# Rotary swap of the retention branch: ScalarE copies between partition quarters instead of permutation products on TensorE

## Chip, cores and metric

The kernel runs on one core of one Trainium2 chip. The metric is the device time of one execution in microseconds (us); the kernel before has a median of 1391.2 us over 3 runs.

## What is computed

Two blocks run one after the other on a sequence of 256 tokens of width 1024, all in float32. The first block is attention beside a recurrence, then a mixture of 32 experts. The second block, where the change lies, has two layers; each projects the normed state into 12 slices of 256 channels, runs four mixers on them and then a feed-forward network:

```python
for l in range(2):
    h = rms_norm(x, norm_mix_pre[l])
    (c_a, c_gate, sb_q, sb_k, sb_v, r_q, r_k, r_v, r_g, sc_b, sc_c, sc_h) = split(h @ w_in[l], 12)
    mix = concat([conformer_conv(c_a, c_gate), stick_breaking_attention(sb_q, sb_k, sb_v),
                  retention(r_q, r_k, r_v, r_g), short_gated_conv(sc_b, sc_c, sc_h)]) @ w_out[l]
    x = x + rms_norm(mix, norm_mix_post[l])
    x = x + rms_norm(conv_ffn(rms_norm(x, norm_ffn_pre[l])), norm_ffn_post[l])

def rotary(x, pos):                      # on r_q and r_k, per head of 64 channels
    x1, x2 = x[..., :32], x[..., 32:]
    return concat([x1 * cos - x2 * sin, x2 * cos + x1 * sin])
```

Channels lie on partitions, so a head's 64 channels are two quarters of 32 partitions. The rotary turn needs `x * cos + swap(x) * sin`, where swap exchanges the two quarters of each head and negates the one that lands in the lower.

## The kernel before

The program is written by hand for each engine (TensorE PE, VectorE DVE, ScalarE ACT, SyncE SP), each with its own list of instructions in the order of the code; semaphores tie them. `layers_part` holds the two layers.

**Projections.** The weight matrices come in pieces of 1 MB (128 partitions x 2048). For each piece ACT rounds the raw weights to `w_hi` (`split_piece`, L2842), DVE makes the rest `w_lo` (`split_low`, L3048), and PE makes a product from `w_hi`*`x_hi`, `w_hi`*`x_lo`, `w_lo`*`x_hi` (`product`, L2700; `values_product`, L2712, for the two v slices; `tokens_product`, L2736, for the output matrix). Piece i uses half-slot i mod 3, so ACT may split piece i when PE has finished piece i-3. Inside a product the part with `w_lo` comes last.

**Order on PE in a layer.** conf_a, conf_gate, sb_q, sb_k, ret_q, the scores of the stick-breaking attention (L2651, L2652), ret_k, ret_v, the two swaps (L2761), the attention's tail sums (L2767 to L2769), sb_v, retention scores from the turned q and k (L2651, L2652 on `o_T`), sc_c, attention output (L2663), sc_h, retention output, sc_b, the group sums ret_mean (L2784), ret_g, ret_var (L2788), conf_mean (L2792), and then the output matrix in rows of pieces (L2736), with conf_var (L2807) after the first.

**The swap.** `m.c("swap")` is a 128x128 permutation with signs; `pe.matmul(ps[b], swap, s_[name])` writes the swapped q or k (128x512) to a PSUM bank. DVE multiplies it with sin (L3112), the slice with cos (L3113), and adds (L3115) into `turned` (the tile `o_T`). Both are done for q, then for k; the second ends with the count 2 of `turned`, for which the retention scores wait. After the turn of k DVE goes on to the tail (L3119), `split_low(8)`, taps of the convolution (L3059), the mask of the retention scores (L3127, L3128), `split_low(9)` for sc_h, and so on.

**PSUM banks.** There are 8 banks of 128x512. `_units` gives every product of a layer a bank before anything runs: the first ones by hand, the middle ones, from conf_gate to conf_var, from a running number n mod 8, and the output matrix and the feed-forward network by hand again:

```python
    for name, count in (("conf_gate", 1), ("sb_q", 1), ("sb_k", 1), ("vec", 1), ("ret_q", 1),
                        ("sb_score", 4), ("ret_k", 1), ("ret_v", 1), ("swap", 2), ("tail", 4), ("sb_v", 1),
                        ...
        for k in range(count):
            use((name, k), n % BANKS)
            n += 1
    for n in range(4):
        use(("out", n), 3 + n)
```

PE calls `free(name)` before it writes a bank; that waits until whoever read the bank's previous use has raised `drained` of the bank (in the listings below `bank_drained2_N`, and `bank_filled2_N` for the count that PE raises). Before the output matrix PE waits for all four of its banks at once: `banks = [free("out", n) for n in range(4)]`. By the table these banks were last used as follows:

| bank of the output matrix | last used by | drained by |
|---|---|---|
| 3 (out 0) | ret_out 0 | ACT copy L2934 |
| 4 (out 1) | ret_out 1 | ACT copy L2934 |
| 5 (out 2) | sc_b | DVE L3158 |
| 6 (out 3) | ret_mean | DVE L3152 |

**ACT between ret_g and the output matrix.** After the product ret_g ACT copies it through SiLU (L2829), loads the table set for Ln and Exp (`preload_act_table_set`, L2939), splits piece 14 (L2842), takes the logarithm of ret_var out of PSUM (L2942), which drains that bank, squares the centred convolution (L2945), and exponentiates (L2947).

## Time and profile before

| | |
|---|---|
| median of 3 runs | 1391.2 us (1389.97 to 1391.92) |
| the profiled execution | 1390.5 us |
| its span, first to last instruction | 1388.6 us |
| instructions | 22573 |
| PE busy | 1186.8 us (85%), 9519 matmuls |
| PEld busy (weight loads, beside PE) | 947.1 us (68%) |
| DVE busy | 743.7 us (54%) |
| ACT busy | 490.3 us (35%) |
| chain that ended last | PE 59%, DMA 16%, DVE 2%, issue 2% |
| layers, from first product to end | 768 to 1388 us |
| mixer of layer 0, of layer 1 | 774 to 881 us, 1082 to 1189 us |

The profile is one execution. Its span leaves out some 2 us around the first and the last instruction. A row of the timeline gives a start, a duration, the engine, line and tiles of a group of like instructions; ends of matmuls are modelled and overlap the next start by about 0.2 us, so distances between starts are what counts on PE. "PEclk" is the clock that TensorE was granted as a share of 2.4 GHz. The experts in the middle of the kernel (340 to 765 us) wait for weights from memory; the layers behind them are ruled by PE.

### The profile page before, as it was taken

Reading aid. Unit: us, or ns where it says so; the run is one execution under the profiler, and the core shown is the slowest. Engines: PE = TensorE matmul, PEld = TensorE weight load, DVE = VectorE, ACT = ScalarE, POOL = GpSimd, SP = SyncE. Lnnn points to the kernel's source line nnn. Section 1 sums busy time; section 2 is a strip of 40 time slices with the busy share of each in tenths; the row PEclk is TensorE's granted clock in tenths of the full one; section 3 lists DMA queues with packets and bytes.
Section 4 is the critical chain, followed back from the end, with each engine's and each line's share of the span. In section 5 each row is a group of like instructions: output and inputs, shape, how many; then the busy total and the mean of one; then the engine's idle time right before and its main releaser. Section 6 shows DMA issues by size and latency. Waiting matters only on the chain.

```text
span 1388.6 us, 22573 instructions
## 1 busy us (share of the span) xinstructions
PE 1186.8 (85%) x9519; PEld 947.1 (68%) x9519; DVE 743.7 (54%) x1148; ACT 490.3 (35%) x674; POOL 2.9 (0%) x12
## 2 busy tenths in 40 slices
PE   7989999999574575736656999999999999999998
PEld 6979798995131221302122898899998998899997
DVE  5484855664010110101001798887777899877776
ACT  4542433422000000000000655744446565744444
POOL 0000000000000000000000000000000000000000
PEclk9999999999786877868688999999999999999999
DMA  8841303799999999999999934576665435676650
GB/s 264 283 132 35 92 4 93 251 404 370 426 427 427 425 426 427 426 426 427 426 425 399 300 123 142 163 216 190 186 182 182 140 119 159 187 204 191 187 152 31
DMA packets 180986, 349.50 MB, mean 252 GB/s; under 512 B 8141, under 2 KB 154738, under 8 KB 167955
## 3 DMA queue, kind: packets, MB, share of 16 engines
q1 hardware_dynamic: 180394, 347.40, 68.9%
q8 instruction: 78, 1.28, 0.4%
q10 hardware_dynamic: 488, 0.62, 0.2%
q14 instruction: 26, 0.21, 0.0%
HBM read 346.93 MB, written 3.43 MB: 252 GB/s over the span
## 4 chain that ended last, share of the span: by engine, by line
PE 59%; DMA 16%; DVE 2%; issue 2%; SPq 1%; ACT 1%; DVEq 1%; ACTq 0%
PE ps L2700 25%; PE ps L2736 11%; DMA expert_ring<-in_w_expert_up 7%; PE ps L1900 6%; DMA expert_top<-in_w_expert_up 4%; PE ps L1931 3%; DMA expert_early<-in_w_expert_up 2%; PE ps L1585 2%; DMA expert_ring<-in_w_expert_gate 2%; PE ps L1888 2%; PE ps L1945 2%; PE ps L2712 2%; PE ps L2674 2%; DMA expert_ring<-in_w_expert_down 1%; SPq L2035 1%
## 5 line engine op out<-in xcount | busy, mean ns | idle before, releaser
L1900 PE MATMUL ps<-expert_ring,w_slot 128*32 128x512 f32 x640 | 118.0, 730 | 101.8 <-DMA expert_ring<-in_w_expert_gate 48.0
L3048 DVE TENSOR_TENSOR w_lo<-expert_early,w_hi 128x2048 fp32r<-128x2048 f32 x80 | 182.8, 2291 | 26.1 <-ACT w_hi L2842 22.8
L1973 DVE TENSOR_TENSOR hT<-ps,hT 128x512 f32<-128x512 f32 x8 | 8.5, 1068 | 346.3 <-PE ps L1900 346.3
L2842 ACT ACTIVATE w_hi<-expert_early 128x2048 fp32r<-128x2048 f32 x80 | 153.0, 1918 | 56.5 <-PE ps L2736 33.8
L1900 PEld LDWEIGHTS ps<-expert_ring,w_slot 128*32 128x32 f32 x640 | 30.8, 131 | 168.9 <-issue 168.9
L2700 PE MATMUL ps<-x_hi,w_hi 128*128 128x256 f32 x960 | 134.2, 282 | 0.0
L2700 PE MATMUL ps<-x_hi,w_lo 128*128 128x256 f32 x960 | 134.2, 282 | 0.0
L2700 PE MATMUL ps<-x_lo,w_hi 128*128 128x256 f32 x960 | 132.3, 280 | 0.0
L2700 PEld LDWEIGHTS ps<-x_hi,w_hi 128*128 128x128 f32 x960 | 122.9, 188 | 3.8 <-issue 1.6
L2700 PEld LDWEIGHTS ps<-x_hi,w_lo 128*128 128x128 f32 x960 | 123.0, 190 | 0.0
L2700 PEld LDWEIGHTS ps<-x_lo,w_hi 128*128 128x128 f32 x960 | 121.0, 188 | 0.0
L3224 DVE SCALAR_TENSOR_TENSOR ff<-ps,ff_taps,ff 128x254 f32<-128x254 f32 (+1 forms) x176 | 76.7, 477 | 47.3 <-ACT ff L2982 43.3
L2982 ACT ACTIVATE ff<-ps,ff_taps 128x256 f32<-128x256 f32 x88 | 36.9, 471 | 118.3 <-PE ps L2700 117.5
L1900 PE MATMUL ps<-expert_early,w_slot 128*32 128x512 f32 x192 | 52.7, 711 | 22.2 <-DMA expert_ring<-in_w_expert_gate 12.6
L1952 ACT ACTIVATE hT<-ps 128x512 f32<-128x512 f32 x8 | 4.8, 597 | 173.0 <-PE ps L1910 173.0
L1900 PE MATMUL ps<-const,w_slot 128*32 128x512 f32 x48 | 37.4, 952 | 32.4 <-DMA expert_early<-in_w_expert_up 21.5
L1950 ACT ACTIVATE hT<-ps 128x512 f32<-128x512 f32 x8 | 4.8, 597 | 154.2 <-PE ps L1900 154.2
L1900 PE MATMUL ps<-expert_top,w_slot 128*32 128x512 f32 x96 | 58.1, 773 | 0.0
L3059 DVE SCALAR_TENSOR_TENSOR att_T<-conf_pad,vec,att_T 128x256 f32<-128x256 f32 x120 | 52.8, 481 | 4.2 <-issue 0.4
L1931 PE MATMUL ps<-expert_ring,hT 128*32 128x512 f32 x288 | 44.3, 620 | 8.7 <-issue 7.3
L2736 PE MATMUL ps<-w_hi,hid_lo 128*128 128x512 f32 x176 | 48.9, 396 | 0.0
L2736 PE MATMUL ps<-w_lo,hid_hi 128*128 128x512 f32 x176 | 48.8, 396 | 0.0
(516 smaller groups left out, 2146.4 us busy)
## 6 DMA issues: line engine op xcount, KB each, us to landing
expert_ring<-in_w_expert_gate SPq DMA_DIRECT2D x22, 2048.0 KB, 28.8
expert_ring<-in_w_expert_up SPq DMA_DIRECT2D x18, 2048.0 KB, 30.0
expert_early<-in_ffn_up SPq DMA_DIRECT2D x36, 1024.0 KB, 6.1
expert_ring<-in_w_expert_down SPq DMA_DIRECT2D x14, 2048.0 KB, 29.8
w_slot<-in_w_in SPq DMA_DIRECT2D x27, 1024.0 KB, 5.5
expert_early<-in_w_in SPq DMA_DIRECT2D x20, 1024.0 KB, 5.6
expert_early<-in_ffn_down SPq DMA_DIRECT2D x18, 1024.0 KB, 5.0
expert_early<-in_w_expert_gate SPq DMA_DIRECT2D x6, 2048.0 KB, 27.5
```

Of the source, the lines that this page charges most:

```text
L1585: mm = pe.matmul(out, w[:, pair_of(i), col:col + P], x[y][:, x0 + k, :], start=(p == 0 and k == 0), stop=(p == 2 and k == n - 1))
L1888: mm = pe.matmul(m.ps[:, b, c * P:(c + 1) * P], m.h_tok[:, t, (4 * j + c) * P:(4 * j + c + 1) * P], picked[:, t, :], start=(t == 0), stop= ...
L1900: mm = pe.matmul(m.ps[rows_of(e), b, :], x_quad[:, k, rows_of(e)], w[e][:, k, :], start=(k == 0), stop=(k == KC - 1))
L1931: mm = pe.matmul(m.ps[rows_of(e), DOWN + j, :], hidden_T[:, f, rows_of(e)], w[e][:, f, j * 512:(j + 1) * 512], start=(f == 0), stop=(f == ...
L1945: pe.matmul(m.ps[:, b, :], gate_T[:, q // 2 * P:(q // 2 + 1) * P], y_quad[:, q % 2 * 512:(q % 2 + 1) * 512], start=True, stop=True).then_i ...
L2700: mm = pe.matmul(m.ps[:, b, j * SEQ:(j + 1) * SEQ], w[:, s, at(k, j):at(k, j) + P], x[:, k, :], start=(part == 0 and k == 0), stop=(part = ...
L2736: mm = pe.matmul(m.ps[:, banks[2 * t + c], :], xs[:, chunk + k, t * P:(t + 1) * P], w[:, s, k * D + c * 512:k * D + (c + 1) * 512], start= ...
L2842: act.activation(w_hi[:, half_slot(l, i), :], raw_slot(m, i), ACT.Copy).then_inc(S["w_hi"], 1)
L2982: ins = act.activation(ff[:, n % 2, j, :], m.ps[:, b, at:at + SEQ], ACT.Copy, scale=ff_taps[:, 2, j * FF + n:j * FF + n + 1])
L3048: dve.tensor_tensor(w_lo[:, s, :], raw_slot(m, i), w_hi[:, s, :].bitcast(F32), ALU.subtract).then_inc(S["w_lo"], 1)
L3059: dve.scalar_tensor_tensor(conf[:, c, :], src, tap, conf[:, c, :], ALU.mult, ALU.add)
L3224: ins = dve.scalar_tensor_tensor(x, m.ps[:, b, at:at + SEQ - back], ff_taps[:, 2 - back, j * FF + n:j * FF + n + 1], x, ALU.mult, ALU.add)
```

## The change

The two swap products leave PE, and their two entries leave the table of banks. ACT makes the swap instead: four activations of 32 partitions x 512 for q after the copy of ret_k, four for k after the copy of ret_v, each from one quarter of the slice to the neighbouring one, with the factor -1 where it lands in a lower quarter. DVE reads the new SBUF tile `swapped` instead of a bank, and waits for the count `swapped`.

```diff
--- before.py
+++ after.py
@@ -2374,7 +2374,7 @@
         use(("conf_a", j), 3 + j)
     n = 1
     for name, count in (("conf_gate", 1), ("sb_q", 1), ("sb_k", 1), ("vec", 1), ("ret_q", 1),
-                        ("sb_score", 4), ("ret_k", 1), ("ret_v", 1), ("swap", 2), ("tail", 4), ("sb_v", 1),
+                        ("sb_score", 4), ("ret_k", 1), ("ret_v", 1), ("tail", 4), ("sb_v", 1),
                         ("ret_score", 4), ("sc_c", 1), ("sb_out", 2), ("sc_h", 1), ("ret_out", 2), ("sc_b", 1),
                         ("ret_mean", 1), ("ret_g", 1), ("ret_var", 1), ("conf_mean", 1), ("conf_var", 1)):
         for k in range(count):
@@ -2501,6 +2501,7 @@
     ret_rs = sb("ret_rs", [P, 2, SEQ])
     ret_o = sb("ret_o", [P, 2, SEQ])
     ret_sq = sb("ret_sq", [P, 2, SEQ])
+    swapped = sb("swapped", [P, 2, 2, SEQ])
     s_ = {n: slices[:, i, :, :] for i, n in enumerate(KEPT)}
 
 
@@ -2512,7 +2513,7 @@
 
     total = {"x_ready": 4, "root": 8, "sum_squared": 8, "scaled": 4, "vec_set": 1, "h_hi": 16, "h_lo": 16, "w_hi": PIECES,
              "w_lo": PIECES, "out_used": 3, "down_used": 10, "y_split": 4, "conf_done": 1,
-             "conf_centred": 1, "conf_squared": 1, "conf_out": 1, "turned": 2, "sb_biased": 4, "soft_ln": 4, "sb_masked": 4,
+             "conf_centred": 1, "conf_squared": 1, "conf_out": 1, "turned": 2, "swapped": 2, "sb_biased": 4, "soft_ln": 4, "sb_masked": 4,
              "sb_arg": 4, "sb_exp": 4, "ret_masked": 4, "ret_centred": 1, "ret_squared": 1, "conf_rooted": 1,
              "ret_rooted": 1, "tap_scaled": FF, "conv_done": FF, "silu_done": FF, "hid_done": FF,
              "conf_normed": 1, "x_half": 2, "half_squared": 2, "half_eps": 2}
@@ -2755,10 +2756,6 @@
             masked_scores("sb_score", s_["sb_k"], s_["sb_q"])
             project("ret_k")
             project("ret_v")
-            for i, name in enumerate(("ret_q", "ret_k")):
-                await_drained(pe, l, name)
-                b = free("swap", i)
-                pe.matmul(m.ps[:, b, :], m.c("swap"), s_[name], start=True, stop=True).then_inc(filled[b], 1)
             if l == 0:
                 pe.wait_ge(m.const_late, 16)
             for h in range(4):
@@ -2913,10 +2910,24 @@
             act.drain()
             for h in range(4):
                 act.activation(sb_l[:, h, :], sb_l[:, h, :], ACT.Ln, bias=1.0).then_inc(S["soft_ln"], 1)
+            def swap_halves(i, name):
+
+                if l > 0:
+                    signalled(act, l - 1, "turned", 2)
+                for r in range(0, P, 32):
+                    low = r % HEAD == 0
+                    src = r + 32 if low else r - 32
+                    ins = act.activation(swapped[r:r + 32, i, :, :], s_[name][src:src + 32, :, :], ACT.Copy,
+                                         scale=-1.0 if low else 1.0)
+                ins.then_inc(S["swapped"], 1)
+
             split_piece(7)
             copy(s_["ret_k"], "ret_k")
+            act.drain()
+            swap_halves(0, "ret_q")
             split_piece(8)
             copy(s_["ret_v"], "ret_v")
+            swap_halves(1, "ret_k")
             split_piece(9)
             for h in range(4):
                 signalled(act, l, "sb_arg", h + 1)
@@ -3108,8 +3119,8 @@
             split_low(7)
             cos, sin = (m.c(n).rearrange("p (o t) -> p o t", o=1).to_broadcast([P, 2, SEQ]) for n in ("cos", "sin"))
             for i, name in enumerate(("ret_q", "ret_k")):
-                b = await_filled(dve, l, "swap", i)
-                dve.tensor_tensor(turn_tmp[:, :, :], two(m.ps[:, b, :]), sin, ALU.mult).then_inc(drained[b], 1)
+                signalled(dve, l, "swapped", i + 1)
+                dve.tensor_tensor(turn_tmp[:, :, :], swapped[:, i, :, :], sin, ALU.mult)
                 dve.tensor_tensor(turned[:, i, :, :], s_[name], cos, ALU.mult)
                 dve.drain()
                 dve.tensor_tensor(turned[:, i, :, :], turned[:, i, :, :], turn_tmp[:, :, :], ALU.add)
```

How the instructions stand. In the listings `bank_drained2_N` and `bank_filled2_N` are the counts of bank N; names such as `rstd_done` or `a_rstd` are those under which an earlier part used the same semaphore, here the layer's own counts (`sb_masked`, `y_split`, `w_hi` and their like).

TensorE at the swap of layer 0, before (the last products are those of ret_v; L2767 to L2769 are the tail):

```order
L2712 MATMUL ps<-w_hi,x_lo 128x256 x8
L2712 MATMUL ps<-w_lo,x_hi 128x256 x8
L2761 MATMUL ps<-slices,const 128x512 [waits bank_drained2_4,bank_drained2_5]
L2761 MATMUL ps<-slices,const 128x512 [waits bank_drained2_5,bank_drained2_2]
L2767 MATMUL ps<-sb_l,const 128x256 [waits bank_drained2_6,rstd_done,const_late]
L2768 MATMUL ps<-sb_l,const 128x128
L2769 MATMUL ps<-sb_l,const 128x128
L2767 MATMUL ps<-sb_l,const 128x256 [waits bank_drained2_7,rstd_done]
```

and with the change:

```order
L2713 MATMUL ps<-w_hi,x_lo 128x256 x8
L2713 MATMUL ps<-w_lo,x_hi 128x256 x8
L2764 MATMUL ps<-sb_l,const 128x256 [waits bank_drained2_4,x_squared,const_late]
L2765 MATMUL ps<-sb_l,const 128x128
L2766 MATMUL ps<-sb_l,const 128x128
L2764 MATMUL ps<-sb_l,const 128x256 [waits bank_drained2_5,x_squared]
```

Two rows with L2761 are gone, and the tail's products go to banks 4 and 5 where they had 6 and 7.

ScalarE at the same place, before (`w_hi` rows split pieces 7, 8 and 9; `slices` rows copy ret_k and ret_v):

```order
L2842 ACTIVATE w_hi<-expert_early 128x2048 [waits bank_filled2_5,landed2_2]
L2829 ACTIVATE slices<-ps 128x512 [waits bank_filled2_2]
L2842 ACTIVATE w_hi<-expert_early 128x2048 [waits bank_filled2_2,landed2_3]
L2829 ACTIVATE slices<-ps 128x512 [waits bank_filled2_3]
L2842 ACTIVATE w_hi<-w_slot 128x2048 [waits bank_filled2_3,landed2_4]
L2923 ACTIVATE w_slot<-w_slot 128x384 [waits x_squared] x4
```

and with the change:

```order
L2839 ACTIVATE w_hi<-expert_early 128x2048 [waits bank_filled2_5,landed2_2]
L2826 ACTIVATE slices<-ps 128x512 [waits bank_filled2_2]
L2920 ACTIVATE swapped<-slices 32x512 x4
L2839 ACTIVATE w_hi<-expert_early 128x2048 [waits bank_filled2_2,landed2_3]
L2826 ACTIVATE slices<-ps 128x512 [waits bank_filled2_3]
L2920 ACTIVATE swapped<-slices 32x512 x4
L2839 ACTIVATE w_hi<-w_slot 128x2048 [waits bank_filled2_3,landed2_4]
L2934 ACTIVATE w_slot<-w_slot 128x384 [waits rows_zero] x4
```

Two groups of four copies stand in; pieces 8 and 9 are split behind them.

TensorE from the variance of retention to the output matrix, layer 0, before:

```order
L2700 MATMUL ps<-x_hi,w_lo 128x256 x8
L2788 MATMUL ps<-ret_sq,const 128x512 [waits bank_drained2_0,vec_in]
L2792 MATMUL ps<-att_T,const 128x256 [waits bank_drained2_1,pads_zero]
L2792 MATMUL ps<-att_T,const 128x256
L2736 MATMUL ps<-w_hi,x_hi 128x512 [waits bank_drained2_6,line_out,bank_drained2_5,a_rstd,bank_drained2_4,bank_drained2_3]
L2736 MATMUL ps<-w_hi,x_hi 128x512 x3
```

and with the change:

```order
L2701 MATMUL ps<-x_hi,w_lo 128x256 x8
L2785 MATMUL ps<-ret_sq,const 128x512 [waits bank_drained2_6,const_in]
L2789 MATMUL ps<-att_T,const 128x256 [waits bank_drained2_7,pads_zero]
L2789 MATMUL ps<-att_T,const 128x256
L2737 MATMUL ps<-w_hi,x_hi 128x512 [waits bank_drained2_6,line_out,bank_drained2_5,a_rstd,bank_drained2_4,bank_drained2_3]
L2737 MATMUL ps<-w_hi,x_hi 128x512 x3
```

The order is the same. What moved is the bank of ret_var: its matmul waited for bank 0 and now for bank 6, and the first product of the output matrix waits, as before, for banks 3 to 6.

ScalarE over the same stretch, before:

```order
L2829 ACTIVATE slices<-ps 128x512 [waits bank_filled2_7]
L2939 ACT_TABLE_LOAD
L2842 ACTIVATE w_hi<-w_slot 128x2048 [waits bank_filled2_7,landed2_4]
L2942 ACTIVATE ret_rs<-ps,const 128x512 [waits bank_filled2_0]
L2945 ACTIVATE conf_sq<-att_T 128x512 [waits w1_lo_done]
```

and with the change:

```order
L2826 ACTIVATE slices<-ps 128x512 [waits bank_filled2_5]
L2950 ACT_TABLE_LOAD
L2839 ACTIVATE w_hi<-w_slot 128x2048 [waits bank_filled2_5,landed2_4]
L2953 ACTIVATE ret_rs<-ps,const 128x512 [waits bank_filled2_6]
L2956 ACTIVATE conf_sq<-att_T 128x512 [waits w1_lo_done]
```

The order is the same; the logarithm of ret_var (`ret_rs<-ps,const`) reads bank 6 where it read bank 0, and it is what drains the bank.

## Rows read from the trace of the kernel before

**Rows 1.** Window, mixer of layer 0: us, busy PE, PEld, DVE, ACT, POOL; PEclk, DMA

```profile
770.00:858.00 88.00, 87.10 (x710) 82.84 (x709) 77.92 (x127) 48.25 (x56) 0.00 (x0) 1.00 0.55 178
```

**Rows 2.** Chain of waits at the swap, both layers: start, us, what

```profile
816.54 1.72 PE ps L2761 x4
...
1124.50 1.72 PE ps L2761 x4
```

**Rows 3.** Timeline of ACT at the swap, layer 0; copy of ret_k, layer 1

```profile
814.33 0.57 ACT L2829 ACTIVATE slices<-ps 128x512 f32<-128x512 f32 x1
...
823.57 0.53 ACT L2923 ACTIVATE w_slot<-w_slot 128x384 f32<-128x384 f32 x1 [4.58 <-DVEq L3121]
...
1121.83 0.57 ACT L2829 ACTIVATE slices<-ps 128x512 f32<-128x512 f32 x1
```

**Rows 4.** Timeline of ACT, prices: four of 384 elements, one of 512

```profile
809.00 1.77 ACT L2912 ACTIVATE sb_l<-sb_l 128x384 f32<-128x384 f32 x4
...
851.81 0.63 ACT L2937 ACTIVATE ret_sq<-ret_o 128x512 f32<-128x512 f32 x1
```

**Rows 5.** Timeline of DVE: turn of k in both layers, then w_lo for sc_h

```profile
820.76 0.69 DVE L3112 TENSOR_TENSOR turn_tmp<-ps,const 128x512 f32<-128x512 f32 x1
...
834.78 2.29 DVE L3048 TENSOR_TENSOR w_lo<-w_slot,w_hi 128x2048 fp32r<-128x2048 f32 x1
...
1128.60 0.69 DVE L3112 TENSOR_TENSOR turn_tmp<-ps,const 128x512 f32<-128x512 f32 x1 [0.47 <-issue]
...
1142.62 2.29 DVE L3048 TENSOR_TENSOR w_lo<-w_slot,w_hi 128x2048 fp32r<-128x2048 f32 x1
```

**Rows 6.** Timeline of PE: first use of that w_lo in sc_h, both layers

```profile
838.42 1.12 PE L2700 MATMUL ps<-x_hi,w_lo 128*128 128x256 f32 x8
...
1146.38 1.12 PE L2700 MATMUL ps<-x_hi,w_lo 128*128 128x256 f32 x8
```

**Rows 7.** Timeline of DVE where it waited for PE: sc_pad, and splitting y

```profile
842.48 0.69 DVE L3136 TENSOR_TENSOR sc_pad<-ps,slices 128x512 f32<-128x512 f32 x1 [0.32 <-PE ps L2700]
...
856.33 0.43 DVE L3035 CAST x_hi<-hT 128x512 fp32r<-128x512 f32 x1 [0.81 <-PE ps L2700]
```

**Rows 8.** Timeline of PE before the output matrix, layer 0, then layer 1

```profile
856.99 1.02 PE L2792 MATMUL ps<-att_T,const 128*128 128x256 f32 x4
857.78 1.17 PE L2736 MATMUL ps<-w_hi,x_hi 128*128 128x512 f32 x4
...
1165.73 1.17 PE L2736 MATMUL ps<-w_hi,x_hi 128*128 128x512 f32 x4
```

**Rows 9.** Timeline of ACT from the copy of ret_g to Ln, both layers

```profile
856.33 0.60 ACT L2829 ACTIVATE slices<-ps 128x512 f32<-128x512 f32 x1 [2.58 <-PE ps L2700]
856.94 1.28 ACT L2939 ACT_TABLE_LOAD   x1
858.24 1.92 ACT L2842 ACTIVATE w_hi<-w_slot 128x2048 fp32r<-128x2048 f32 x1
860.06 0.67 ACT L2942 ACTIVATE ret_rs<-ps,const 128x512 f32<-128x512 f32 x1
...
1168.02 0.67 ACT L2942 ACTIVATE ret_rs<-ps,const 128x512 f32<-128x512 f32 x1
```

**Rows 10.** Windows over pauses of PE and what followed, columns as in rows 1

```profile
100.70:103.30 2.60, 0.00 (x0) 0.00 (x0) 2.56 (x2) 0.00 (x0) 0.00 (x0) 1.00 0.01 2
103.30:108.50 5.20, 5.18 (x27) 4.72 (x27) 4.88 (x9) 0.00 (x0) 0.00 (x0) 0.67 0.17 28
...
138.90:140.40 1.50, 0.02 (x1) 0.05 (x1) 0.42 (x2) 0.06 (x1) 0.06 (x1) 1.00 0.38 40
140.40:145.00 4.60, 4.60 (x22) 4.06 (x23) 4.43 (x6) 2.16 (x3) 0.25 (x1) 1.00 0.64 215
286.20:288.40 2.20, 0.01 (x2) 0.01 (x1) 2.04 (x4) 1.62 (x1) 0.00 (x0) 1.00 0.98 417
288.40:292.50 4.10, 4.10 (x22) 4.10 (x22) 3.93 (x5) 0.00 (x0) 0.00 (x0) 0.58 1.03 440
```

## Prediction, made before the changed kernel was timed

> **What bounds the kernel here.** I read the page first: shares of busy time and the chain that ended last. The layers come after the experts, and in that chain they are one piece of PE work after another. So I cut out the mixer. Over 88 us of layer 0 PE is busy for 87.1, DVE for 77.9 and ACT for 48.3, at the full clock [rows 1]. PE is the bound, DVE runs close behind it, ACT has room. The chain of waits says the same of the swap: its products lie on the path with 1.72 us in each layer [rows 2]. What is taken from PE is gained in full only as long as DVE and ACT, and the PSUM banks that they give back, are never late. So I went through the timeline of all three engines behind the swap, and through every wait of PE there by the table of banks.
>
> **What goes.** Two products of 128x512 in each layer, four matmul records, 1.72 us on the chain [rows 2]: 2 x 1.72 = 3.4 us, if nothing takes their place. DVE's multiplication with sin reads SBUF instead of PSUM. That costs nothing either way, since the row from PSUM takes 0.69 us and the reader is not at fault for the wait that follows.
>
> **What comes on ACT.** Eight activations of 32 partitions x 512 per layer. No row shows one that crosses partition quarters. The nearest: one of 512 elements takes 0.63 us, and four of 384 take 1.77 us, so 0.41 from start to start with 0.53 for the last [rows 4]. The 0.10 us between 0.53 and 0.63 goes on top of the step: 0.52. A group of four is then 3 x 0.52 + 0.63 = 2.2 us. From below I take the step of the 384 row (1.8 us), from above four with no overlap (2.5 us), and I stay with 2.2, which comes from rows of the same engine and length. Fewer partitions I count as no saving.
>
> These 2 x 2.2 us fit into ACT's idle time. Behind these splits ACT waited 4.58 us for DVE [rows 3]. But the group for k comes late: the copy of ret_k ends at 814.90 [rows 3], then group q to 817.1, the split of piece 8 (1.92 us, the row of such a split in rows 9) to 819.0, the copy of ret_v to 819.45, group k to 821.55, each start overlapping the end before by 0.1. DVE began the turn of k at 820.76 [rows 5]; now it waits until about 821.57, **0.8 us late**. In layer 1 the copy of ret_k starts at 1121.83 [rows 3], 307.5 later, so group k ends at 1129.05, and DVE, which began at 1128.60 [rows 5], is **0.5 us late**. Queued behind that wait on DVE are the tail, w_lo of sc_c, taps, the masks and w_lo of sc_h; none can be skipped, and DVE has no idle time in between.
>
> **First place where that meets PE: sc_h.** w_lo of sc_h was done at 834.78 + 2.29 = 837.07 [rows 5], and PE first used it at 838.42 [rows 6]: 1.35 us of slack. PE now comes 1.72 earlier (836.70) and w_lo 0.8 later (837.87). With 0.05 us for the signal PE waits 1.2 and keeps 0.5 of its 1.72. In layer 1 w_lo was done at 1144.91 and used at 1146.38 [rows 5, 6]: now 1145.4 against 1144.66, a wait of 0.8, and 0.9 is kept. The same comparison at sc_c, the product before it, where the slack was 3.0 us, leaves 0.5. The retention scores need both turns at about 825.7 and have them at 823.7.
>
> **Second place: the output matrix, by way of the banks.** Taking two entries out of a running number mod 8 moves every later product two banks down, while the output matrix keeps banks 3 to 6 by hand. ret_var had bank 0 and now has bank 6, which is bank "out 3". PE asks for all four banks before the first row of the output matrix, and bank 6 is now given back by ACT's logarithm of ret_var. Both PE and ACT start from the same event here, the end of the product ret_g. PE came to the output matrix at 857.78 [rows 8]. ACT copies ret_g at 856.33, loads a table (1.28), splits piece 14 (1.92), and ends the logarithm at 860.06 + 0.67 = 860.73 [rows 9]. With the signal PE can start at 860.78, so it waits **3.0 us** more than before. In layer 1 the logarithm ends at 1168.69 and PE came at 1165.73 [rows 8, 9]: 3.0 again. Nothing that is gained ahead of ret_g helps, since the race begins at its end. DVE's work for the first row of the matrix was due before that and gets slack from it; after it PE runs as before, and the rest of the layer hangs on PE.
>
> The table load stands in this race. Its row shows 1.28 us with the next instruction 0.02 later [rows 9]. The Trainium skill (ScalarE: Activation LUTs, "What ACT_TABLE_LOAD costs") puts a drain of about 1.38 us behind every load. By that the logarithm would end some 1.4 us later, and the sum below would be 2.7 us higher. The row shows no such drain, so it is left out.
>
> **Third: TensorE's clock.** PE's last product before the matrix ends at 858.01 [rows 8], so the new pause is 860.78 - 858.01 = 2.8 us. The trace has two pauses of like length: 2.6 us, after which the granted clock averaged 0.67 over 5.2 us, and 2.2 us, after which it was 0.58 over 4.1 us; after one of 1.5 us it stayed at 1.00 [rows 10]. A fall is to 1.2 of 2.4 GHz, and costs 5.2 x 0.33 = 1.7 us or 4.1 x 0.42 = 1.7 us of PE's work. The new pause is longer than both that were followed by a fall, so I count **1.7 us** per layer. From below it is nothing, if the fall does not come.
>
> **The sum.** Layer 0: -1.72 + 1.2 + 3.0 + 1.7 = +4.2. Layer 1: -1.72 + 0.8 + 3.0 + 1.7 = +3.8. Together **+8.0 us**. The profiled execution took 1390.5 us (span 1388.6), so it would become 1398.5. The median shown is 1391.2, 0.7 above it, and on that footing the time is **1399.2 us**, 0.6% slower. With groups of 1.8 us DVE is not late: 1.3 and 1.4 us are kept and the sum is +6.7. With 2.5 us DVE is 1.4 and 1.1 late: PE's waits at sc_h are 1.8 and 1.4, nothing and 0.3 are kept, and the sum is +9.2. So the forecast's own range is 1398 to 1400.4, and 1397 to 1401 with the scatter of a median of three.
>
> **Rivals.**
> (1) *The bank wait, but no fall of the clock.* For it: the layers show no fall at all so far [rows 1], and whether one comes may depend on more than the length of the pause. Against: both longer pauses of rows 10 were followed by one. +8.0 - 3.4 = +4.6, so 1395.8. One fall of two gives 1397.5.
> (2) *The other side: bank 6 is free in time.* The mechanism is the cover behind ret_g. If ACT's logarithm ended 3.0 us sooner after ret_g, PE would not stop, and there would be no pause for the clock either. For it: rows 2, where the gain is plain. Against: the chain of four instructions in rows 9 has no idle time to shrink, and the listing shows the wait on bank 6 in front of the matrix. It decides when copy, load, split and logarithm take under 1.65 us together, where the rows have 4.4. Then 0.5 + 0.9 us stay, 1389.8, or a little less, because DVE had only 0.32 + 0.81 us of idle time to give up [rows 7] before its splitting of y holds PE. If ACT's copies cost DVE nothing either, the gain is 1.3 + 1.4 = 2.7 us, and 1387.8 where sc_h has slack too.
> (3) *Copies between quarters are dearer than any row here.* One us more per group makes DVE 2 us later in each layer and sc_h waits 2 longer: +4 us, 1403. Against: the rows of ACT go by elements per partition, and nothing in them speaks of where a result lands.
> That the swap's products stay on PE after all is excluded by the listing.
>
> **How the numbers follow.** Forecast 0.74; no fall, or one of two, 0.13; copies much dearer 0.05; bank free in time 0.08. A measurement of this kernel can tell about 0.2%, 2.8 us, from no change. Slower by more than that: the first three, 0.92. Within it: 0.05, and faster 0.03, the two parts of rival 2. The range goes from below rival 1 to the top of the forecast: 1395.2 to 1401.2; outside it lie rivals 2 and 3, 0.13, and little of the rest.
>
> **What the profile after would show.** In each layer, a new idle time of about 2.8 us on PE in front of L2737, released by ACT's `ret_rs` (L2953); behind it a stretch of PEclk at half; a wait of about 1 us in sc_h for w_lo; DVE waiting 0.4 to 0.8 us for ACT at the turn of k; groups of four on ACT of 2.2 us. I am wrong if PE has no idle time before the output matrix, or if the clock holds over it.

## The result, and the profile after

The changed kernel took 1403.7 us (1399.05 to 1404.46, 5 runs) where the kernel before, on the same chip, took 1391.92 us (1389.97 to 1392.85, 5 runs): a ratio of 1.0082 with an interval from 1.0071 to 1.0092, slower. A second set of 6 runs of it gave 1401.1 us and 1.0067 (1.0052 to 1.0081). The forecast was 1399.2 with a range up to 1401.2. So the direction was right and the size too small: by 4.5 us against the first median, which lies outside the range, and by 1.9 against the second, which lies just inside it.

The profiled execution took 1401.57 us, which is 11.1 above that of before (1390.5). The page of the kernel after (busy time and instructions of each engine; the chain that ended last):

```profile
span 1399.7 us, 22571 instructions
...
PE 1187.8 (85%) x9511; PEld 949.4 (68%) x9511; DVE 744.0 (53%) x1148; ACT 500.5 (36%) x690; POOL 2.9 (0%) x12
...
PE 50%; DMA 16%; DVE 6%; ACT 3%; issue 3%; DVEq 2%; SPq 1%; ACTq 0%
```

ACT carries 10.2 us more (490.3 before), which is four groups of four copies at 2.55. PE has eight matmul records fewer and is yet not less busy. Part of the chain has moved from PE (59% before) to DVE and ACT (2% for DVE before): PE now waits for them.

**Where the time went.** I cut each layer's mixer at four points of PE's timeline that both kernels have: the start of the layer (its products with `scale_eye`, which transpose the state), the start of ret_var, the first row of the output matrix, and the end of that matrix. Times in us, layer 0 / layer 1, from the starts of the rows:

| stretch of PE | before | after | difference | predicted |
|---|---|---|---|---|
| A: first product to ret_var | 86.79 / 85.70 | 87.42 / 86.17 | +0.63 / +0.47 | -0.5 / -0.9 |
| B: ret_var to the output matrix | 1.65 / 1.64 | 4.95 / 4.96 | +3.30 / +3.32 | +3.0 / +3.0 |
| C: the output matrix | 23.47 / 23.56 | 24.84 / 24.92 | +1.37 / +1.36 | +1.7 / +1.7 |

That is +10.5 us in the mixers, where the forecast had +8.0. The rest of the 11.1 is nearly all ahead of the layers (0.55 us, in code that did not change). The evidence follows, stretch by stretch.

**Stretch A.** ACT's timeline at the swap of layer 0, and the group for q in layer 1 (start, us, engine, line, tiles, count of instructions in the row, idle time before it and what ended it):

```profile
814.89 0.57 ACT L2826 ACTIVATE slices<-ps 128x512 f32<-128x512 f32 x1
815.54 2.55 ACT L2920 ACTIVATE swapped<-slices 32x512 f32<-32x512 f32 x4
818.11 1.91 ACT L2839 ACTIVATE w_hi<-expert_early 128x2048 fp32r<-128x2048 f32 x1
819.93 0.58 ACT L2826 ACTIVATE slices<-ps 128x512 f32<-128x512 f32 x1
820.53 2.55 ACT L2920 ACTIVATE swapped<-slices 32x512 f32<-32x512 f32 x4
...
1128.69 2.55 ACT L2920 ACTIVATE swapped<-slices 32x512 f32<-32x512 f32 x4 [0.36 <-issue]
```

A group takes 2.55 us, not 2.2: four times 0.64 one behind the other. It does not overlap its neighbours either: the split starts at 818.11, 0.02 after the group's end, and the second group 0.02 after the end of the copy. The starts of ret_k's copy lie where they did ([rows 3] plus the 0.55 us from before the layers). On DVE the turn of k then waits:

```profile
823.11 0.69 DVE L3123 TENSOR_TENSOR turn_tmp<-swapped,const 128x512 f32<-128x512 f32 x1 [1.91 <-ACT swapped L2920]
...
837.14 2.29 DVE L3059 TENSOR_TENSOR w_lo<-w_slot,w_hi 128x2048 fp32r<-128x2048 f32 x1
...
844.44 0.69 DVE L3147 TENSOR_TENSOR sc_pad<-ps,slices 128x512 f32<-128x512 f32 x1
...
1136.28 0.69 DVE L3123 TENSOR_TENSOR turn_tmp<-swapped,const 128x512 f32<-128x512 f32 x1 [2.20 <-ACT swapped L2920]
```

The turn of k began at 820.76 before [rows 5]; with 0.55 us for the code ahead of the layers that is 821.31, so DVE is 1.8 us late. It is still 1.8 late at w_lo of sc_h (834.78 in rows 5, plus 0.55, against 837.14). The idle time that DVE had before sc_pad [rows 7] is used up. PE meets this twice in each layer, in sc_c and in sc_h:

```profile
830.42 1.22 PE L2701 MATMUL ps<-x_hi,w_lo 128*128 128x256 f32 x8 [0.34 <-DVE w_lo L3059]
...
839.49 1.21 PE L2701 MATMUL ps<-x_hi,w_lo 128*128 128x256 f32 x8 [1.42 <-DVE w_lo L3059]
...
1143.59 1.21 PE L2701 MATMUL ps<-x_hi,w_lo 128*128 128x256 f32 x8 [0.19 <-DVE w_lo L3059]
...
1152.66 1.21 PE L2701 MATMUL ps<-x_hi,w_lo 128*128 128x256 f32 x8 [1.42 <-DVE w_lo L3059]
```

Of the 1.72 us that left PE, none is kept. A group of eight that starts after a wait has its next group 1.05 us behind it instead of 0.95, and the idle time shown is less than the gap between starts, since ends of matmuls are modelled. Starts are the safe reading.

**Stretch B.** PE before the output matrix, layer 0, then layer 1:

```profile
857.32 1.02 PE L2785 MATMUL ps<-ret_sq,const 128*128 128x512 f32 x2
858.18 1.03 PE L2789 MATMUL ps<-att_T,const 128*128 128x256 f32 x4
862.27 1.70 PE L2737 MATMUL ps<-w_hi,x_hi 128*128 128x512 f32 x4 [3.07 <-ACT ret_rs L2953]
863.78 1.91 PE L2737 MATMUL ps<-w_hi,x_lo 128*128 128x512 f32 x4
...
1175.45 1.18 PE L2737 MATMUL ps<-w_hi,x_hi 128*128 128x512 f32 x4 [3.07 <-ACT ret_rs L2953]
```

and ACT's chain that ends the wait:

```profile
857.52 0.60 ACT L2826 ACTIVATE slices<-ps 128x512 f32<-128x512 f32 x1 [1.82 <-PE ps L2701]
858.13 1.28 ACT L2950 ACT_TABLE_LOAD   x1
859.43 1.91 ACT L2839 ACTIVATE w_hi<-w_slot 128x2048 fp32r<-128x2048 f32 x1
861.24 0.67 ACT L2953 ACTIVATE ret_rs<-ps,const 128x512 f32<-128x512 f32 x1
```

The four instructions are those of [rows 9] with the same durations, and the logarithm's end, 861.91, releases PE. Behind the table load the next instruction starts 0.02 us after its end, as it did before. The drain of some 1.38 us that the Trainium skill (ScalarE: Activation LUTs, "What ACT_TABLE_LOAD costs") adds to a load is again not seen, neither there nor ahead of the load, which starts 0.01 us after the end of the copy. PE does not start 0.05 us after the logarithm but 0.36.

**Stretch C.** The granted clock in a window of 6 us behind the start of the output matrix, each layer (us, then busy time of PE, PEld, DVE, ACT, POOL, then PEclk, DMA share, GB/s):

```profile
862.00:868.00 6.00, 5.72 (x18) 4.59 (x19) 5.70 (x8) 1.07 (x2) 0.00 (x0) 0.72 0.81 221
1176.00:1182.00 6.00, 6.00 (x21) 4.76 (x20) 4.99 (x7) 0.32 (x1) 0.00 (x0) 0.72 0.94 262
```

The granted clock averaged 0.72 in both, where the kernel with the banks put back, below, has 1.00: it fell in both layers. The rows of four products of 128x512 show it as well: 1.91 us for the row at 863.78, over which the granted clock was 0.50 (1.2 GHz), where the kernel with the banks put back has 1.10 at 2.4 GHz.

### The profile page after: what moved, and what is told of

Its sections match the earlier page's. It is cut to its first block, busy times and chain, and to the rows that moved or that the text cites. A ratio compares the mean times of both kernels' runs of the same rounds, so it can differ in the third digit from the quotient of the medians.

```text
span 1399.7 us, 22571 instructions
## 1 busy us (share of the span) xinstructions
PE 1187.8 (85%) x9511; PEld 949.4 (68%) x9511; DVE 744.0 (53%) x1148; ACT 500.5 (36%) x690; POOL 2.9 (0%) x12
## 4 chain that ended last, share of the span: by engine, by line
PE 50%; DMA 16%; DVE 6%; ACT 3%; issue 3%; DVEq 2%; SPq 1%; ACTq 0%
PE ps L2701 20%; PE ps L2737 11%; DMA expert_ring<-in_w_expert_up 7%; PE ps L1900 6%; DMA expert_top<-in_w_expert_up 4%; PE ps L1931 4%; DMA expert_early<-in_w_expert_up 2%; PE ps L1585 2%; DMA expert_ring<-in_w_expert_gate 2%; PE ps L1888 2%; PE ps L1945 2%; PE ps L2675 2%; DVE w_lo L3059 1%; DVE att_T L3070 1%; DMA expert_ring<-in_w_expert_down 1%
## 5 line engine op out<-in xcount | busy, mean ns | idle before, releaser
L1900 PE MATMUL ps<-expert_ring,w_slot 128*32 128x512 f32 x640 | 114.6, 710 | 99.8 <-DMA expert_ring<-in_w_expert_gate 47.4
```

Of the source, the lines that this page charges most:

```text
L1900: mm = pe.matmul(m.ps[rows_of(e), b, :], x_quad[:, k, rows_of(e)], w[e][:, k, :], start=(k == 0), stop=(k == KC - 1))
```

## Experiments on the three steps

**The banks put back.** The two numbers that the swap had used are skipped, so every product has the bank it had before; the copies stay on ACT.

```diff
-                        ("sb_score", 4), ("ret_k", 1), ("ret_v", 1), ("tail", 4), ("sb_v", 1),
+                        ("sb_score", 4), ("ret_k", 1), ("ret_v", 1), ("skipped", 2), ("tail", 4), ("sb_v", 1),
...
-            use((name, k), n % BANKS)
+            if name != "skipped":
+                use((name, k), n % BANKS)
```

> The change with the old bank numbers: two numbers are skipped where the swap's products stood, so ret_var is back in bank 0. Theory (late w_lo from ACT's copies, plus bank 6, plus the clock): the wait of 3.3 us before the output matrix and the fall of the clock behind it are gone in both layers, only DVE's lateness stays (start of ret_g's end +0.6 and +0.5 us against the kernel before). So +1 to +1.5 us against the kernel before, about 1393. Rival (ACT's copies themselves and the waits for w_lo make most of it, banks do not matter): stays within 2 us of the changed kernel, +9 us or more.

Measured: 1391.63 us (11 runs) against 1390.74 (21 runs of the kernel before, shared with the next two experiments and with "k before piece 8"), ratio 1.0009 (1.0000 to 1.0018). In the trace B is 1.71 / 1.69 and C 23.48 / 23.56 as before, A is 87.42 / 86.18 as in the changed kernel. PE's timeline where the changed kernel stood still, and the two windows:

```profile
857.30 1.03 PE L2790 MATMUL ps<-att_T,const 128*128 128x256 f32 x4
858.15 1.17 PE L2738 MATMUL ps<-w_hi,x_hi 128*128 128x512 f32 x4
859.16 1.10 PE L2738 MATMUL ps<-w_hi,x_lo 128*128 128x512 f32 x4
```

```profile
862.00:868.00 6.00, 6.00 (x28) 4.90 (x27) 5.66 (x10) 3.13 (x5) 0.00 (x0) 1.00 0.93 260
1176.00:1182.00 6.00, 6.00 (x27) 4.86 (x26) 5.80 (x6) 5.48 (x6) 0.00 (x0) 1.00 0.68 184
```

So B and C come from the order of the banks alone, and they are nearly nine tenths of the loss. What is left, +1.2 us in the mixers, is the copies' own cost: moving the swap to ACT gains nothing in this form even with the banks right.

**The bank alone.** The kernel before, swap products and all, with one entry of the table changed: ret_var gets bank 6.

```diff
-            use((name, k), n % BANKS)
+            use((name, k), 6 if name == "ret_var" else n % BANKS)
```

> The kernel before, swap on TensorE, with one thing changed: ret_var is put in bank 6 by hand. Theory: PE waits 3.3 us for ACT's logarithm before the output matrix in each layer, and the clock falls behind it for 1.4 to 1.7 us: +9.4 us, about 1401. Without the fall of the clock +6.6. Rival (banks do not matter): no difference.

Measured: 1399.11 us (5 runs), ratio 1.0058 (1.0044 to 1.0071). A 86.80 / 85.75, B 4.95 / 4.95, C 24.82 / 24.94: +4.66 and +4.74 us in the two mixers. One number in a table costs 9.4 us of the trace in a kernel where the swap was not touched. PE's timeline there:

```profile
861.06 2.04 PE L2736 MATMUL ps<-w_hi,x_hi 128*128 128x512 f32 x4 [3.07 <-ACT ret_rs L2942]
```

The first experiment's +1.2 and this one's +9.4 add up to the changed kernel's +10.5 within 0.2: the two parts hardly influence each other.

**The pause without its idleness.** The changed kernel with three further products of constants between conf_mean and the output matrix, into the bank that conf_var overwrites afterwards.

```diff
+            b = free("conf_var")
+            for _ in range(3):
+                pe.matmul(m.ps[:, b, :], m.c("ones"), m.c("iota"), start=True, stop=True)
             banks = [free("out", n) for n in range(4)]
```

> The change as it is, banks shifted, with three products of constants (0.86 us each) into the free bank of conf_var while PE waits before the output matrix. Theory: the wait for ACT's logarithm stays (5.0 us from ret_var to the output matrix), but the idle piece of it is under 1 us and the clock holds at 1.00: 1.4 us a layer less, -2.8 us against the changed kernel. Rival (the slow products behind the wait have another cause, such as transfers of weights): no difference to the changed kernel.

Measured: 1398.14 us (5 runs), ratio 1.0054 (1.0040 to 1.0068). B is 4.95 / 4.95 as without the products, C 23.31 / 23.40: the clock stays up, and 1.53 / 1.52 us come back against the changed kernel.

```profile
858.73 2.74 PE L2794 MATMUL ps<-const 128*128 128x512 f32 x6
861.96 1.18 PE L2737 MATMUL ps<-w_hi,x_hi 128*128 128x512 f32 x4 [0.50 <-ACT ret_rs L2956]
862.98 1.09 PE L2737 MATMUL ps<-w_hi,x_lo 128*128 128x512 f32 x4
```

The price of the fall was taken at 1.7 and is 1.5. That it is a cost of its own, beside the wait, is shown, and not by this experiment alone: in the kernel of "all 128 partitions", below, which has no such products, B is 4.95 in both layers, the clock held in layer 0 and C is 23.31 there, against 24.84 in the changed kernel. C at the full clock is 0.16 us shorter than in the kernel before (23.47 / 23.56), because its first row takes 2.87 us instead of 3.02 when PE comes to it late; so C grew by 1.4 against before, although the fall costs 1.5.

**One warm product instead of three.** The same edit with a single product, to shorten the idle part of the pause from 3.07 to some 2.2 us.

> e4 with one product of constants in place of three, which leaves a pause of about 2.2 us on PE before the output matrix. The pauses of 3.1 us were followed by a fall of the clock in every trace, that of 0.5 us was not; in the kernel before a pause of 2.2 us was. I expect the fall, so 1.4 us more from output matrix to turn than in e4, and the time of the changed kernel; if it holds at 1.00, the time of e4.

Measured: one run, 1401.39 us; the pause is 2.24 / 2.21 and the clock fell in both layers (C 24.86 / 24.93, PEclk 0.72 in the windows of stretch C):

```profile
862.10 1.68 PE L2737 MATMUL ps<-w_hi,x_hi 128*128 128x512 f32 x4 [2.24 <-ACT ret_rs L2955]
```

So the clock can fall after a pause of 2.2 us, as in the last two rows of [rows 10]. That it does not always fall is shown by the next run.

**The 0.3 us behind the logarithm.** PE waits for the four banks first, and the waits for the split y and for w_hi of piece 14 stand behind them, although their data are there long before. Here, in the kernel of "the bank alone", they go ahead of the waits for the banks:

```diff
+            signalled(pe, l, "y_split", 1)
+            await_split(pe, l, "w_hi", PIECE_OUT)
             banks = [free("out", n) for n in range(4)]
             for r, t in ((0, None), (1, None), (2, 0), (3, 0), (2, 1), (3, 1)):
                 tiles = range(TT) if t is None else (t,)
-                if t != 1:
+                if t != 1 and r > 0:
                     signalled(pe, l, "y_split", r + 1)
```

(and `tokens_product` leaves out its own wait for that w_hi).

> e2 (swap on TensorE, ret_var in bank 6) with PE's waits for y and for w_hi of the output matrix's first piece put ahead of the waits for its banks. In e2 the first product starts 0.3 us after ACT's logarithm ends. Theory (PE takes the two waits left behind that for bank 6 one after the other): it starts 0.1 to 0.2 us sooner. Rival (the delay lies between ACT's end and the count of the bank): unchanged, within 0.05 us. The time is that of e2 within 0.6 us.

Measured: one run, 1397.16 us, 2.0 under "the bank alone" and not within 0.6 of it. The logarithm ends at 860.84 + 0.67 = 861.51 and PE starts 0.15 us later instead of 0.36; B is 4.74 in both layers instead of 4.95:

```profile
861.66 1.18 PE L2736 MATMUL ps<-w_hi,x_hi 128*128 128x512 f32 x4 [2.85 <-ACT ret_rs L2944]
```

Waits that are already met still take PE's time when they stand behind the one that is not: some 0.2 us here for two. What nothing had led me to expect is the clock: after this pause of 2.85 us it stayed at 1.00 in both layers (C 23.32 / 23.39), though it fell after 2.2 in the run above. Against C of "the bank alone" that is 3.05 us in the trace, more than the time came out below what was expected. The window in layer 0:

```profile
862.00:868.00 6.00, 6.00 (x28) 4.89 (x27) 5.39 (x7) 0.67 (x2) 0.00 (x0) 1.00 0.93 254
```

## Experiments on the price of the copies

**Does the crossing cost?** The changed kernel with each copy made from its own quarter (`src = r`); the exchange of the halves is left out.

```diff
-                    src = r + 32 if low else r - 32
+                    src = r
```

> The changed kernel with every copy of 32 partitions staying in its own quarter (so the swap itself is left out and the turn is computed from unswapped slices). Each copy took 0.64 us with no overlap, where four whole-tile activations of 384 elements overlap by 0.12. Theory A (crossing quarters costs the overlap): groups of four take 2.2 us. Theory B (a write to fewer partitions, or this operation, does): groups stay at 2.55 us. No expectation for the time beyond: with A about 1 us less than the changed kernel, with B the same.

Measured: one run, 1400.25 us, and both groups of layer 0 take what they took, 2.55 and 2.54. The first group, then the copy of ret_v and the second:

```profile
814.53 2.55 ACT L2920 ACTIVATE swapped<-slices 32x512 f32<-32x512 f32 x4
...
818.92 0.58 ACT L2826 ACTIVATE slices<-ps 128x512 f32<-128x512 f32 x1
819.40 2.54 ACT L2920 ACTIVATE swapped<-slices 32x512 f32<-32x512 f32 x4
```

Inside a group, crossing from one quarter to another is not the cause, and rival 3's mechanism falls. In front of a group it does make a difference. The second group here starts 0.10 us before the copy ahead of it has ended (0.10 in layer 1 too), where the changed kernel's starts 0.02 behind it. The first copy of the group now reads and writes the first quarter; in the changed kernel it reads the second and writes the first.

**All 128 partitions.** For q alone, four copies of the whole slice, to four tiles; the exchange is left out for q. The group for k is as in the changed kernel.

```diff
+                    if i == 0:
+                        dst = (swapped[:, i, :, :], ret_sq[:, :, :], ret_o[:, :, :], ret_rs[:, :, :])[r // 32]
+                        ins = act.activation(dst, s_[name], ACT.Copy, scale=-1.0 if low else 1.0)
+                        continue
```

> The changed kernel with the four copies for q as copies of all 128 partitions to four different tiles (so the swap of q is left out), those for k as they are. If these four take 2.2 us beside 2.55 for k's, activations of whole tiles overlap and those of 32 partitions don't; if both take 2.55, the overlap is missing for another reason, such as the length or the operation. The time should be that of the changed kernel within 0.7 us.

Measured: one run, 1398.61 us. That is 2.5 us under the changed kernel run again and not within 0.7: A is 0.47 / 0.48 shorter and the clock held in layer 0, which is 1.5. The copies start 0.52 us apart, which is the step that the prediction took, and the split behind them starts 0.10 before the last has ended; the group for k stays at 2.55 in the same run:

```profile
815.08 0.63 ACT L2922 ACTIVATE swapped<-slices 128x512 f32<-128x512 f32 x1
815.61 0.62 ACT L2922 ACTIVATE ret_sq<-slices 128x512 f32<-128x512 f32 x1
...
816.66 0.61 ACT L2922 ACTIVATE ret_rs<-slices 128x512 f32<-128x512 f32 x1
817.17 1.90 ACT L2839 ACTIVATE w_hi<-expert_early 128x2048 fp32r<-128x2048 f32 x1
...
819.58 2.55 ACT L2924 ACTIVATE swapped<-slices 32x512 f32<-32x512 f32 x4
```

Left open by it: is it the number of partitions, or that they change from one copy to the next?

**32 partitions, always the same.** For q four copies of 32 partitions, all from and to the first quarter of four tiles, and one whole copy behind them; the exchange is left out for q.

```diff
+                    if i == 0:
+                        dst = (swapped[0:32, i, :, :], ret_sq[0:32, :, :], ret_o[0:32, :, :], ret_rs[0:32, :, :])[r // 32]
+                        ins = act.activation(dst, s_[name][0:32, :, :], ACT.Copy, scale=-1.0 if low else 1.0)
+                        if r == 96:
+                            act.drain()
+                            ins = act.activation(swapped[:, i, :, :], s_[name], ACT.Copy)
+                        continue
```

> The changed kernel with q's four copies of 32 partitions all in the first quarter, into four different tiles, followed by one whole-tile copy so that the turn finds data (the swap of q is left out). Theory A (an activation waits for the one before when it works on other partitions): start to start 0.52 us, as with whole tiles. Theory B (activations of 32 partitions never overlap): 0.64 us.

Measured: one run, 1400.11 us:

```profile
815.66 0.63 ACT L2922 ACTIVATE swapped<-slices 32x512 f32<-32x512 f32 x1
816.20 0.61 ACT L2922 ACTIVATE ret_sq<-slices 32x512 f32<-32x512 f32 x1
...
817.24 0.61 ACT L2922 ACTIVATE ret_rs<-slices 32x512 f32<-32x512 f32 x1
...
820.86 2.56 ACT L2927 ACTIVATE swapped<-slices 32x512 f32<-32x512 f32 x4
```

Copies of 32 partitions overlap by 0.1 us too when they stay on the same partitions. The step from one to the next is 0.52 us on the same partitions, whether 32 or 128, and 0.64 where the partitions change. Both experiments also write to four tiles where the change writes to one, but that is not the difference: the four activations of [rows 4] work in one tile and overlap, and the split behind a group of the change works in other tiles and does not. The Trainium skill (ScalarE: Activation LUTs, "What ACT_TABLE_LOAD costs", which has a paragraph on ACTIVATE itself) states, for an activation with immediate scale and bias, 186 ns plus 0.833 ns per element, and an overlap of about 93 ns between activations in a row; for 512 elements that is an estimate of 0.61 us and of a step of 0.52. The rows agree with that for one activation (0.61 to 0.63 us) and for the step on unchanged partitions (0.52), and not for the kernel's own groups, where there is no overlap. Why the overlap is lost, the runs do not show.

## Experiments on a better order

**k before piece 8.** The banks as before, and the copies for k directly behind those for q.

```diff
             swap_halves(0, "ret_q")
+            swap_halves(1, "ret_k")
             split_piece(8)
             copy(s_["ret_v"], "ret_v")
-            swap_halves(1, "ret_k")
```

> e1 (old banks) with the four copies for k directly behind those for q, ahead of the split of piece 8. Eight copies of 0.64 us end about 820.2 on the clock of the kernel before, where DVE turned k at 820.76, so DVE is not late. Theory: PE waits 0.4 us at sc_h, keeps 1.3 us, and DVE's idle time (0.32 + 0.81) caps the gain at 1.1 to 1.3 us a layer: -2.4 us against the kernel before, about 1389.5, and 3.6 us under e1. Rival (removing PE work gains nothing here, since DVE's total work bounds the mixer): within 0.5 us of the kernel before.

Measured: 1388.99 us (11 runs), ratio 0.9987 (0.9978 to 0.9996); mixers -1.06 / -1.23 us. DVE's turn of k no longer waits for ACT. PE keeps 1.11 and 1.25 of its 1.72 us (A); most of the rest goes into a smaller wait for w_lo of sc_h:

```profile
836.28 1.21 PE L2702 MATMUL ps<-x_hi,w_lo 128*128 128x256 f32 x8 [0.28 <-DVE w_lo L3060]
```

**And w_lo of sc_h before the masks.** In addition DVE makes `split_low(9)` ahead of the masks of the retention scores, which the retention output needs only after sc_h.

```diff
             conf_taps(18, 22)
+            split_low(9)
             for h in range(4):
                 b = await_filled(dve, l, "ret_score", h)
...
-            split_low(9)
```

> e3 with DVE's w_lo for sc_h moved ahead of the mask of the retention scores, 3.0 us earlier. Theory (DVE's total work up to the end of ret_g caps the mixer): PE no longer waits in sc_h, but y and its w_lo come no sooner, so PE waits that much in front of the output matrix instead; within 0.3 us of e3 in the mixers, about -2.3 us against the kernel before. Rival (the wait in sc_h is what keeps the rest of the gain back): PE keeps all 1.72 us per layer, -3.4 us.

Measured: 1388.93 us (12 runs) against 1391.63 (17 runs of before), ratio 0.9979 (0.9971 to 0.9988). This version is faster than both kernels. The waits in sc_c and sc_h are gone, and A is -1.70 / -1.69, the whole of the swap. The mixers as a whole gain only 1.09 / 1.19 us, since PE now waits at the output matrix for DVE:

```profile
856.87 0.69 DVE L3049 TENSOR_TENSOR x_lo<-hT,x_hi 128x512 fp32r<-128x512 f32 x1
...
857.82 1.17 PE L2738 MATMUL ps<-w_hi,x_hi 128*128 128x512 f32 x4 [0.35 <-DVE x_lo L3049]
```

That is the end of DVE's slack which rival 2 named [rows 7]: 1.1 us in layer 0. The two orders cannot be told apart: the intervals of their ratios overlap, and the mixers of both gain 2.3 us in sum. What PE gains ahead of the output matrix beyond DVE's slack, it gives back there.

**The changed kernel again**, unchanged, because the first median stood 2 us above its own profiled execution.

> The changed kernel once more, beside more runs of the kernel before. The traces account for 10.5 us of it in the two mixers; the five runs of the first comparison gave 11.8 us. Theory: 10.5 us is all there is, and the rest is scatter, so +9.5 to +11.5 us. Rival (executions in which the clock falls more often or for longer than in the profiled one): +11.5 us or more again.

Measured: 1401.1 us (1399.25 to 1401.66, 6 runs) against 1391.63 (17 runs): +9.5 us, where the first set gave +11.8. The two intervals of the ratio overlap between 1.0071 and 1.0081. So about 1 us of the first difference either way is scatter, and the traced +10.5 in the mixers lies between the two.

## Why the prediction came out as it did

**What bounds the kernel, and the swap's 1.72 us.** Right. The moved products were worth 1.70 us per layer to PE where nothing took their place (A in "w_lo of sc_h before the masks").

**The copies on ACT.** This is the step that failed. The prediction put a group at 2.2 us, with a step of 0.52, and let each start overlap the end before by 0.1. It named 2.5 as the bound "with no overlap" and went by the rows of whole tiles, which all stay on the same 128 partitions. The group takes 2.55. In layer 0 the miss adds up from the rows: 2 x 0.35 for the groups, 0.2 for the overlaps with the split behind the first and the copy ahead of the second, which are lost as well, and 0.08 in front of the first group, where the code has a drain. Together 1.0 us, and DVE is 1.8 us late instead of 0.8. In layer 1 there is the same 0.9 and 0.36 of issue time in front of the first group: 1.75 late instead of 0.5, after the 5.93 us that the code before it had lost. What makes the 0.36 stays open; this layer's code has a wait for the turns of the layer before in front of each group, but the second group starts 0.02 us behind its copy all the same. The sum's own upper case, groups of 2.5 us, allowed 0.6 us more lateness, not 1.0 and 1.25, because it let the neighbours go on overlapping and had nothing in front of the first group.

**PE at sc_h.** The mechanism and the place were right, and the arithmetic holds with the measured lateness: 1.35 us of slack, less 1.72, less 1.81, is a shortfall of 2.2 us, which PE pays in sc_c and sc_h together (the prediction saw 0.5 left at sc_c, and with 1.0 more lateness that is gone too). A came out 1.15 and 1.39 us above the forecast: 1.0 and 1.25 of it DVE, and some 0.15 in each layer beside it, of which the slower first group after a wait in sc_h is 0.1. That is 2.5 us of the missing size.

**The wait for bank 6.** Right in place, cause and nearly in size: 3.3 instead of 3.0 in each layer. The 0.3 is the time that PE needs after the last signal: 0.36 us, not 0.05. (At sc_h, where PE waits for one signal only, the 0.05 holds: w_lo ends at 839.43 and PE starts at 839.49.) Two further waits stand behind that for the banks, and when they went ahead of it 0.2 came back. That is 0.6 us of the missing size.

**The clock.** It fell in both layers as forecast, and C grew by 1.4 us each instead of 1.7, so 0.7 us was too much. The prediction multiplied the length of a window by the missing clock. The same product gives 6.0 x 0.28 = 1.7 in the windows of the changed kernel, where the fall costs 1.5 between starts: the product overstates what PE loses by some 0.15. The other 0.16 is what PE gains back in C by coming late. That both layers had a fall in the trace was in part luck: pauses of the same length were followed by none in 2 of 12 cases, below.

**The sum.** +8.0 + 2.5 + 0.6 - 0.7 = +10.4, and +10.5 was measured in the mixers. The upper bound of the copies had allowed +1.2 of the 2.5 us that they and what they delay cost; seen in full, that step alone would have given 1399.2 + 2.5 = 1401.7, above the range.

**The rivals.** (1) no fall of the clock: not what the changed kernel did, and worth 3.05 us where three products filled most of the pause. (2) the bank free in time: what it said, 1389.8 if 0.5 + 0.9 us stay, is the experiment with the banks put back. That kernel came out 0.9 us above before and not 1.4 below, since the 0.5 + 0.9 are not kept. Its other figure, 2.7 us of gain where the copies cost DVE nothing, was then reached by changes of order: 1.8 and 2.7 by the medians, 2.3 by the mixers. DVE's slack in front of the output matrix sets that limit, as the prediction had it. (3) copies between quarters dearer: its effect was there with a third of its size, 0.35 us per group, and inside the group not by the crossing.

## What to carry over

A bank table that is filled by a running number ties every later product to the entries before it. Taking two entries out cost 9.4 us here, where the edit's own part cost 1.2; leave the numbers as holes, or look up for each bank that is used by hand who drains it now. When work goes from the engine that bounds the kernel to another, it pays only as far as the engines between them have slack. Reckon that slack from the next use of each thing they make, move those makers forward too (here the copies of k and one w_lo), and price short instructions on changing partitions without the overlap that rows on unchanged partitions show.

## What the hardware showed that was not expected

**Activations that step from partition to partition lose their overlap.** From start to start 0.52 us for copies of 512 elements on the same partitions (32 or 128 of them), 0.64 where they move on to another quarter. The neighbours of a group show what counts. The split behind a group never overlaps it (0.02 us behind its end). The copy of 128 partitions ahead of the second group is overlapped by 0.10 us when the group begins by reading and writing the first quarter, in both layers of "Does the crossing cost?", and not when it begins by reading the second (0.02 behind). So going from 128 partitions to 32 does not by itself cost the overlap. What all these rows have in common is that two activations overlap where both start at the same partition, in what they read and in what they write; that is read from them and was not tested by a run of its own.

**The length of a pause does not by itself decide on the clock.** Before the output matrix, with the same program around it: with 3.07 us idle it fell in 10 of 12 pauses (both layers of six traces: the changed kernel twice, "the bank alone", and the three experiments on the price of the copies); with 2.85 us in none of 2; with 2.24 and 2.21 in both; with 0.50 in none of 2. One trace could show both: with whole-tile copies of q it held in layer 0 and fell in layer 1, with 32 partitions always the same it fell in layer 0 and held in layer 1. The two windows of each of these kernels:

```profile
861.30:867.30 6.00, 5.99 (x26) 4.89 (x27) 5.51 (x8) 0.81 (x2) 0.00 (x0) 1.00 0.86 240
1175.00:1181.00 6.00, 6.00 (x23) 4.82 (x22) 3.04 (x6) 0.22 (x1) 0.00 (x0) 0.80 0.92 239
```

```profile
862.60:868.60 6.00, 6.00 (x19) 4.76 (x20) 5.50 (x7) 0.79 (x2) 0.00 (x0) 0.72 0.87 240
1176.00:1182.00 6.00, 6.00 (x29) 4.88 (x27) 5.18 (x7) 0.51 (x1) 0.00 (x0) 1.00 0.92 255
```

So after a pause of 2 to 3 us a fall is possible here, and it costs 1.5 us of PE's time, but a single trace doesn't tell which way it goes. What decides is left open. The forecast's certainty on this term was too high, though the term came true.

**Waits that are met are not free behind one that is not.** PE started 0.36 us after the last signal with two met waits behind it, and 0.15 us with them ahead of it.
